# Attention scores beside the Fourier products, Hyena tables in pieces, and the experts' first block by products on TensorE

## Chip, cores and metric

The kernel runs on one core of one Trainium2 chip. The metric is the device time of one execution in microseconds: the median of several runs. Everything is computed in float32; large products are split into a high and a low part (fp32r), and three products of the parts are summed.

## The reference

Two transformer blocks, one after the other, on 512 tokens of width 1024.

- `first_block` has two layers and 256 further context tokens. Each layer takes one input projection and mixes it in three ways: attention over 8 query heads and 2 key heads (512 columns), a Fourier mix (256 columns: a 2-D DFT, then a 256x256 product), and a Hyena long convolution (256 columns: DFT of the signal and of a filter, product, inverse DFT). The output projection, a gated residual and a convolutional FFN follow. Gates and shifts come from a modulation product of the condition vector.
- `second_block` has one attention layer and a mixture of experts: each token picks one of 4 groups and 2 of its 4 experts.

```
g_weight, g_idx = lax.top_k(softmax(xf @ w_group + b_group), 1)
e_val, e_idx = lax.top_k(e_in_group, 2)
combine = sum(one_hot(expert_id) * softmax(e_val) * g_weight)
act = silu(xf @ w_gate[e]) * (xf @ w_up[e]) * combine[:, e]
out = sum over e of act @ w_down[e]
```

## The kernel before

It is written for the five engines with an explicit semaphore for every dependence; each engine executes its own list in order.

**Weights.** SyncE fetches all weight slabs (128x1024) through a ring of three (`wraw`). ScalarE makes `whi`, GpSimd `wlo` (L578), TensorE multiplies. Slabs of the modulation lie in the same ring; TensorE uses them directly in pairs (`hy_pair`, L743), and SyncE refills a slot when it is used.

**A layer's mixers.** After the input projection TensorE does the Fourier mix: L911 (`fst2`, 24 products in layer 0, 16 in layer 1), L921 (`fst3`), then the transposes of the values (L928). ScalarE evacuates to `fy` and to `hhi`; ScalarE and VectorE make `vth` and `vtl` of the values (L1570, L2126 to L2128). Attention then runs in steps, one of 128 queries against all keys of one head: `scores(i)` computes steps i and i+1 (L945), VectorE takes the minimum (L2140), ScalarE the exponential (L1585), VectorE or ScalarE divides by the sum (L2151, L1623), TensorE transposes the probabilities (L956), ScalarE and VectorE split them into `pth` and `ptl` (L1596, L2159), and TensorE multiplies by the values (L970). Loops handle two steps at a time: `scores(i)` stands ahead of `transposed(i-2)`, the outputs that are due, and `transposed(i-1)`.

**Hyena.** When attention's last output is out, ScalarE issues the tables on its own queue: `hyf512` (2 MB, into `hd5`), `hyi512` (2 MB, `hi5`) and in layer 0 `hy256` (1 MB). TensorE does `hy_pair(0)`, transposes the signal, does `hy_pair(1)` and then for each quarter of the frequencies the filter's products (L1017) and the signal's (L1029), with further pairs between them, and at the end the inverse (L1050).

**Experts.** Tokens are sorted by group into 7 blocks of 128 rows. VectorE computes the group, the place of each token (`slot_i`) and the experts' weights. GpSimd scatters the 512 rows of `xrow` to DRAM by place (L602), waits until they are there, loads block 0 (L605) and blocks 1 to 6 (L607) to `xs`, and only then starts on its share of the weight cuts (`mlo`, L611): slab 1 of experts 1 to 3 of each block. TensorE transposes block 0 (L1289), VectorE and ScalarE make `hT`, `hTh` and `hTl`, and the units start: one unit is one expert of one block, with 6 weight slabs. In a unit TensorE does `gate_up` (L1319, slabs 0 to 3) with the transposes of the last unit's activations in it (`turn_act`, L1297, behind slab 1) and `down2` of the last unit (L1337). SyncE fetches each 512 KB slab into a ring of ten (L561), ScalarE makes `mhi` (L1811), VectorE most of `mlo` (L2519).

Of the kernel before, what the change touches and what calls it, by code (L numbers as in the profile page):

```python
# [29 lines left out]
P = 128  # L30
# [118 lines left out]
def program(nc, dram, out):  # L149
# [132 lines left out]
    below = sb("below", [P, P], headones_o)  # L282
    xrow = sb("xrow", [P, TX // P, ROW], BIG)
# [19 lines left out]
    aTl = sb("aTl", [P, 2, DEXP], SCR + 13312, F32R)  # L303

# [260 lines left out]
    def _(pool):  # L565
# [9 lines left out]
        for n in range(N_SLABS):  # L575
# [13 lines left out]

            if n == B2_SLAB + IN2_T + RING - 1:  # L590
# [9 lines left out]
        pool.wait_ge(sem("routed"), 4)  # L600
# [20 lines left out]
    def _(pe):  # L621
# [174 lines left out]
        for L in range(DEPTH):  # L796
# [105 lines left out]
            pe.wait_ge(sem("fab_ready"), T // P * L + ntt)  # L902
            pe.wait_ge(sem("k_roped"), 5 * L + 5)
            for f in range(2):
                for s, c0, nt_ in fseg:
                    w = nt_ * P
                    dst = ps[:, 6 + f, 0:w] if s == 0 else ps[:, 5 - f, 0:w]
                    tb = fl5 if s == 0 else fl2
                    for q in range(nt_):
                        for ab in range(2):  # L910
                            m = pe.matmul(dst, fab[:, c0 // P + q, ab * 256 + f * P:ab * 256 + f * P + P],  # L911
                                          tb[:, ab, q, 0:w], start=q == 0 and ab == 0, stop=q == nt_ - 1 and ab == 1)
                    m.then_inc(sem("fst2"), 1)

            pe.wait_ge(sem("fy_ready"), 4 * L + 2 * len(fseg))
            for o in range(2):
                for s, c0, nt_ in fseg:
                    w = nt_ * P
                    dst = ps[:, 6 + o, 0:w] if s == 0 else ps[:, 5 - o, 0:w]
                    for f in range(2):  # L920
                        m = pe.matmul(dst, wfo[:, f, o * P:o * P + P], fy[:, f, c0:c0 + w], start=f == 0, stop=f == 1)  # L921
                    m.then_inc(sem("fst3"), 1)

            pe.wait_ge(sem("k_roped"), 5 * L + 5)
            pe.wait_ge(sem("four_out"), 4 * L + 2 * len(fseg))
            pe.wait_ge(sem("qk_lo"), 5 * L + 5)
            for tt in range(6):
                m = pe.transpose(ps[:, 4 + tt // 4, (tt % 4) * P:(tt % 4) * P + P], pxq[:, PXV, tt * P:tt * P + P],  # L928
                                 ident[:, :])
# [47 lines left out]
            for i in range(0, max(shares) + 1, 2):  # L977
                if i < N:
                    scores(i)
# [1788 lines left out]
```

## Time and profile before

| | |
|---|---|
| median of 3 runs | 2558.72 us (2557.14 to 2561.62) |
| the profiled execution | 2567.32 us, span 2565.5 us, granted clock 0.951 |
| TensorE, VectorE, ScalarE, GpSimd busy | 91%, 50%, 43%, 25% |
| chain that ended last | TensorE 77%, VectorE 12%, ScalarE 3%, DMA 2% |
| last four of 40 slices | VectorE 9, 9, 9, 8 tenths; 342, 346, 348, 270 GB/s |
| `mlo` on VectorE (L2519) | 147 x 1.451 us |
| `mlo` on GpSimd (L611) | 21 x 3.014 us |

A timeline row has the start and the duration in us, the engine, the line, the operation with its operands and count, and in brackets the idle time ahead of it with what ended it. SPq and ACTq are DMA issues on SyncE's and ScalarE's queues. A row of the chain has start, duration and the work or wait that the end went back to. A row of windows has, for each engine in the order TensorE, its weight loads, VectorE, ScalarE, GpSimd, the busy time; then the granted clock (1.00 is 2.4 GHz), the share in which the DMA engines were busy, and GB/s.

### The profile page before, as it was taken

To read this page: it belongs to the slowest core of one execution; us is meant where nothing else is said; L and a number is where in the kernel's file an instruction comes from. 1 tells how busy PE (TensorE), PEld (TensorE's weight loads), DVE (VectorE), ACT (ScalarE), POOL (GpSimd) and SP (SyncE) were. 2 spreads that over 40 slices of the span, in tenths; PEclk is the share of its full clock that TensorE was granted. 3 is DMA by queue.
4 is the path that set the end of the run, shared out by engine and by line. 5 is a ranking of instruction groups with operands and counts; after the bars stand their busy time and mean duration, and the time that the engine had idled before them with its cause. 6 is when DMAs were issued, how large, how long until landed. Compare 5 with 4: busy or idle time off the path is not lost.

```text
span 2565.5 us, 32207 instructions
## 1 busy us (share of the span) xinstructions
PE 2334.2 (91%) x12378; PEld 1861.8 (73%) x12378; DVE 1289.5 (50%) x2035; ACT 1096.9 (43%) x1687; POOL 652.5 (25%) x293
## 2 busy tenths in 40 slices
PE   4997979979999999988979888999999999959997
PEld 2875856858888788866657566888876877747776
DVE  3565932053431344236667214534524269449998
ACT  4323931353332333225357035434423268437776
POOL 1220000242222222242200034444444410212223
PEclk9999989979999999988989888999999999979999
DMA  6520032113222232112400441333332322249997
GB/s 239 190 89 22 1 117 98 58 30 118 91 66 66 83 114 75 58 50 94 140 1 33 153 144 55 94 98 98 98 97 68 100 66 59 109 162 342 346 348 270
DMA packets 81034, 291.20 MB, mean 114 GB/s; under 512 B 10713, under 2 KB 13050, under 8 KB 79932
## 3 DMA queue, kind: packets, MB, share of 16 engines
q1 hardware_dynamic: 74192, 257.68, 29.8%
q10 hardware_dynamic: 4108, 22.08, 2.3%
q0 software_dynamic: 2592, 9.48, 0.9%
q8 instruction: 96, 1.57, 0.2%
q14 instruction: 46, 0.38, 0.0%
HBM read 283.43 MB, written 9.48 MB: 114 GB/s over the span
## 4 chain that ended last, share of the span: by engine, by line
PE 77%; DVE 12%; ACT 3%; DMA 2%; issue 2%; POOL 2%; DVEq 1%; SPq 0%; ACTq 0%; POOLq 0%
PE ps L635 37%; PE ps L682 12%; DVE mlo L2519 5%; PE ps L658 3%; PE ps L970 3%; PE ps L956 2%; PE ps L1319 2%; PE ps L743 2%; PE ps L1191 2%; PE ps L945 1%; POOL x L584 1%; PE ps L1017 1%; PE ps L911 1%; PE ps L1337 1%; PE ps L1029 1%
## 5 line engine op out<-in xcount | busy, mean ns | idle before, releaser
L578 POOL TENSOR_TENSOR wlo<-wraw,whi 128x1024 fp32r<-128x1024 f32 x208 | 502.1, 2415 | 1530.0 <-ACT whi L1359 881.1
L635 PE MATMUL ps<-hhi,whi 128*128 128x512 f32 x1624 | 593.6, 366 | 3.0 <-DVE hlo L2219 2.0
L635 PE MATMUL ps<-hlo,whi 128*128 128x512 f32 x1624 | 585.3, 360 | 0.0
L635 PE MATMUL ps<-hhi,wlo 128*128 128x512 f32 x1624 | 582.5, 359 | 0.0
L635 PEld LDWEIGHTS ps<-hhi,whi 128*128 128x128 f32 x1624 | 307.6, 189 | 83.6 <-issue 31.2
L635 PEld LDWEIGHTS ps<-hhi,wlo 128*128 128x128 f32 x1624 | 306.6, 189 | 48.1
L635 PEld LDWEIGHTS ps<-hlo,whi 128*128 128x128 f32 x1624 | 307.4, 189 | 45.7 <-issue 1.0
L1942 DVE SCALAR_TENSOR_TENSOR up<-ps,cconv,up 128x511 f32<-128x511 f32 (+1 forms) x132 | 83.2, 658 | 296.3 <-ACT up L1686 293.8
L2519 DVE TENSOR_TENSOR mlo<-mraw,mhi 128x1024 fp32r<-128x1024 f32 x147 | 208.9, 1451 | 5.3 <-ACT mhi L1811 5.2
L1366 ACT ACTIVATE whi<-wraw 128x1024 fp32r<-128x1024 f32 x132 | 138.9, 1052 | 154.2 <-PE ps L682 120.3
L1686 ACT ACTIVATE up<-ps,cconv 128x768 f32<-128x768 f32 (+1 forms) x88 | 77.8, 885 | 257.6 <-PE ps L635 257.2
L682 PE MATMUL ps<-alo,whi 128*128 128x512 f32 (+1 forms) x528 | 188.0, 356 | 0.0
L682 PE MATMUL ps<-ahi,whi 128*128 128x512 f32 (+1 forms) x528 | 187.4, 355 | 0.0
L682 PE MATMUL ps<-ahi,wlo 128*128 128x512 f32 (+1 forms) x528 | 186.6, 353 | 0.0
L1811 ACT ACTIVATE mhi<-mraw 128x1024 fp32r<-128x1024 f32 x168 | 166.0, 1049 | 1.2 <-DMA mraw<-in_w_moe 1.0
L2268 DVE TENSOR_TENSOR y<-y,ps 128x768 f32<-128x768 f32 (+1 forms) x32 | 26.3, 820 | 227.6 <-PE ps L682 227.6
L1359 ACT ACTIVATE whi<-wraw 128x1024 fp32r<-128x1024 f32 x76 | 80.2, 1057 | 112.3 <-PE ps L635 86.9
L682 PEld LDWEIGHTS ps<-ahi,whi 128*128 128x128 f32 x528 | 99.6, 189 | 15.0
L682 PEld LDWEIGHTS ps<-ahi,wlo 128*128 128x128 f32 x528 | 99.2, 188 | 14.8
L611 POOL TENSOR_TENSOR mlo<-mraw,mhi 128x1024 fp32r<-128x1024 f32 x21 | 63.3, 3014 | 183.1 <-ACT mhi L1811 183.1
L682 PEld LDWEIGHTS ps<-alo,whi 128*128 128x128 f32 x528 | 99.5, 188 | 13.8
L658 PE MATMUL ps<-hhi,whi 128*128 128x512 f32 (+1 forms) x168 | 68.1, 405 | 32.4 <-DVE hlo L1920 22.9
(350 smaller groups left out, 4185.6 us busy)
## 6 DMA issues: line engine op xcount, KB each, us to landing
wraw<-in_w_all SPq DMA_DIRECT2D x288, 512.0 KB, 3.6
mraw<-in_w_moe SPq DMA_DIRECT2D x168, 512.0 KB, 5.5
mraw_b<-in_w_mod SPq DMA_DIRECT2D x10, 512.0 KB, 15.4
fl<-in_four ACTq DMA_DIRECT2D x2, 2048.0 KB, 8.2
hd<-in_hyf ACTq DMA_DIRECT2D x2, 2048.0 KB, 10.0
hi<-in_hyi ACTq DMA_DIRECT2D x2, 2048.0 KB, 15.8
slot_rows<-in_slot_rows ACTq DMA_DIRECT2D x1, 3612.0 KB, 20.6
xs<-slot_rows POOLq DMA_DIRECT2D x7, 516.0 KB, 7.2
```

Of the source, the lines that this page charges most:

```text
L578: pool.tensor_tensor(wlo[:, slot, :], wraw[:, AT_W[n] % RING, :], whi[:, slot, :].bitcast(F32), ALU.subtract).then_inc(lo_split, 1)
L611: pool.tensor_tensor(mlo2[:, n % MS, :], mraw2[:, n % MR, :], mhi2[:, n % MS, :].bitcast(F32), ALU.subtract).then_inc(pool_lo, 1)
L635: m = pe.matmul(ps[:, bank + b, 0:w], a, r[:, c0:c0 + w], start=k == 0 and q == 0, stop=k == KT - 1 and q == 2)
L658: m = pe.matmul(ps[:, bank + b, 0:w], a, r[:, c0:c0 + w], start=k == 0 and q == 0, stop=k == KT - 1 and q == 2)
L682: m = pe.matmul(ps[:, bank + b, 0:w], a, r[:, c0:c0 + w], start=k == 0 and z == 0, stop=k == PAIRS - 1 and z == 2)
L970: m = pe.matmul(ps[:, 6 + ht % 2, c0:c0 + HALF], u[:, g, kts[c], :], w[:, unit % 2, c, g * HALF:g * HALF + HALF], start=g == 0 and c == 0 ...
L1359: act.activation(whi[:, n % RING, :], wraw[:, AT_W[n] % RING, :], ACT.Copy).then_inc(hi_split, 1)
L1366: act.activation(whi[:, n % RING, :], wraw[:, AT_W[n] % RING, :], ACT.Copy).then_inc(hi_split, 1)
L1686: act.activation(up[:, p % 2, z, 0:W], psf[:, b * 512:b * 512 + W], ACT.Identity, bias=cconv[:, s, 3:4], scale=cconv[:, s, 1:2]).then_inc( ...
L1811: act.activation(mhi2[:, m % MS, :], mraw2[:, n % MR, :], ACT.Copy).then_inc(ring_hi, 1)
L1942: dve.scalar_tensor_tensor(dst[:, c0 + 1:c0 + w], ps[:, bank + b, 0:w - 1], w0, dst[:, c0 + 1:c0 + w], ALU.mult, ALU.add)
L2519: dve.tensor_tensor(mlo2[:, m % MS, :], mraw2[:, n % MR, :], mhi2[:, m % MS, :].bitcast(F32), ALU.subtract).then_inc(ring_lo, 1)
```

## The change

Three things are moved or replaced.

1. In each layer the scores, minima and exponentials of attention's steps 0 to 3 stand between and behind the two halves of L911 and their evacuations, ahead of L921 and the value transposes. The first pair is scaled there too. The main loop starts at i = 2 and computes scores from i = 4.
2. In layer 0 three of four parts of `hyf512` are loaded by GpSimd's queue while attention runs on the context queries (after 8 units of outputs); ScalarE loads the last quarter at the end of attention. In both layers `hyi512` is issued behind the first `hsp` copy, `hy256` behind the second.
3. The first block of sorted rows is no longer taken from DRAM. VectorE compares each token's place with 0 to 127 (`iota`, loaded over `rot`); TensorE forms the transposed block as products of `xrow` with these 0/1 matrices, and the rows' weights likewise, which go to `meta0`. The rows' way through DRAM stays, for all 7 blocks; block 0 from DRAM is waited for only where its result is added.

```diff
+            if n == IN_T + RING - 1:
+                pool.wait_ge(sem("o_ready"), 2 * NQT)
+                pool.dma_start(hd5[:, 0, 0:2, :], dram["hyf512"][:, 0, 0:2, :]).then_inc(sem("hfwd_early"), 16)
+                pool.dma_start(hd5[:, 1, :, :], dram["hyf512"][:, 1, :, :]).then_inc(sem("hfwd_early"), 16)
...
         pool.wait_ge(sem("slots_clear"), 16)
-        pool.wait_ge(sem("routed"), 4)
+        pool.wait_ge(sem("routed"), 5)
...
             for f in range(2):
                 for s, c0, nt_ in fseg:
...
                     m.then_inc(sem("fst2"), 1)
+                if f == 0:
+                    pe.wait_ge(sem("qk_lo"), 5 * L + 5)
+                scores(2 * f)
...
-            for i in range(0, max(shares) + 1, 2):
-                if i < N:
+            for i in range(2, max(shares) + 1, 2):
+                if 4 <= i < N:
                     scores(i)
...
                 pe.wait_ge(sem("hfwd_in"), 16 * L + 16)
+                pe.wait_ge(sem("hfwd_early"), 32)
...
+        def place_first(half, bank):
+            if half == 0:
+                pe.wait_ge(sem("routed"), 4)
+            for q in range(4):
+                k = 4 * half + q
+                for tt in range(TX // P):
+                    m = pe.matmul(ps[:, bank, q * P:q * P + P], xrow[:, tt, k * P:k * P + P], place1[:, tt, :],
+                                  start=tt == 0, stop=tt == TX // P - 1)
+            m.then_inc(sem("hT_done"), 1)
+        def place_weights():
+            pe.wait_ge(sem("routed"), 5)
+            for tt in range(TX // P):
+                m = pe.matmul(ps[:, 4, 0:ROW - D], place1[:, tt, :], xrow[:, tt, D:ROW], start=tt == 0,
+                              stop=tt == TX // P - 1)
+            m.then_inc(sem("hT_done"), 1)
...
-        turn_block(0, 0, 7)
-        turn_block(0, 1, 6)
+        place_first(0, 7)
+        place_first(1, 6)
+        place_weights()
...
+            for f in range(2):
+                for s, c0, nt_ in fseg:
...
+                    act.activation(fy[:, f, c0:c0 + w], ps[:, 6 + f, 0:w] if s == 0 else ps[:, 5 - f, 0:w],
+                                   ACT.Copy).then_inc(sem("fy_ready"), 1)
+                exponentials(2 * f)
+                exponentials(2 * f + 1)
+                if f == 0:
+                    scaled_act(1)
...
             act.wait_ge(sem("attn_out"), 2 * NQT * L + nht)
-            act.dma_start(hd5[:, :, :, :], dram["hyf512"]).then_inc(sem("hfwd_in"), 16)
-            act.dma_start(hi5[:, :, :, :], dram["hyi512"]).then_inc(sem("hinv_in"), 16)
             if L == 0:
-                act.dma_start(hd2[:, :, :, :], dram["hy256"]).then_inc(sem("hinv_in"), 16)
+                act.dma_start(hd5[:, 0, 2:4, :], dram["hyf512"][:, 0, 2:4, :]).then_inc(sem("hfwd_in"), 16)
+            else:
+                act.dma_start(hd5[:, :, :, :], dram["hyf512"]).then_inc(sem("hfwd_in"), 16)
...
                     act.activation(hsp[:, f, :], ps[:, 4 + f % 2, :], ACT.Copy).then_inc(sem("hsp_ready"), 1)
+                    if s == 0 and f == 0:
+                        act.dma_start(hi5[:, :, :, :], dram["hyi512"]).then_inc(sem("hinv_in"), 16)
+                    if L == 0 and s == 0 and f == 1:
+                        act.dma_start(hd2[:, :, :, :], dram["hy256"]).then_inc(sem("hinv_in"), 16)
...
+            minimum(0)
+            minimum(1)
+            scaled(0)
+            scaled(1)
+            minimum(2)
+            minimum(3)
...
         dve.tensor_copy(slot_i[:, :], r(8, 1, 10).rearrange("p t n -> p (t n)"))
+        for tt in range(TX // P):
+            m = dve.tensor_scalar(place1[:, tt, :], iota[:, :], rt[:, 8, tt, 10:11], None, ALU.is_equal)
+        m.then_inc(sem("routed"), 1)
...
             c = 2 + 2 * (b % 2)
+            if b == 0:
+                dve.wait_ge(sem("first_block_in"), 16)
...
         block_full(0, 0, 7)
         block_full(0, 1, 6)
+        dve.wait_ge(sem("hT_done"), 3)
+        dve.tensor_copy(meta0[:, :], ps[:, 4, 0:ROW - D])
+        dve.drain()
         block_low(0, 0)
         block_low(0, 1)
```

## Rows read from the trace of the kernel before

**Rows 1.** Timeline of TensorE, layer 0, from the Fourier products to full attention.
```profile
231.50 5.43 PE L921 MATMUL ps<-fy,wfo 128*128 128x512 f32 x16 [0.47 <-ACT fy L1555]
237.91 0.85 PE L928 MATMUL ps<-ident,pxq 128*128 128x128 f32 x6 [0.98 <-issue]
...
247.07 1.54 PE L956 MATMUL ps<-ident,pr 128*128 128x128 f32 x6 [2.77 <-DVE pr L2151]
249.42 1.52 PE L956 MATMUL ps<-ident,pr 128*128 128x128 f32 x6 [0.80 <-DVE ptl L2159]
...
256.97 0.51 PE L945 MATMUL ps<-hhi 64*128 64x512 f32 x2 [0.32 <-ACT pr L1585]
```

**Rows 2.** Timelines of ScalarE and of VectorE in the same stretch.
```profile
242.82 0.87 ACT L1570 ACTIVATE vth<-ps 128x384 fp32r<-128x384 f32 x2
...
243.83 0.38 DVE L2126 MEMSET vth<- 128x384 f32 x1 [1.95 <-ACT vth L1570]
...
245.76 0.49 DVE L2128 TENSOR_TENSOR vtl<-ps,vth 128x384 fp32r<-128x384 f32 x1
...
253.29 1.82 DVE L2140 TENSOR_REDUCE stat<-ps 128x1 f32<-128x768 f32 x2 [0.95 <-PE ps L945]
```

**Rows 3.** Windows, layer 0, ahead of the first transposes.
```profile
240.00:244.20 4.20, 1.24 (x14) 0.97 (x12) 2.20 (x3) 2.63 (x6) 0.00 (x0) 1.00 0.00 0
244.20:247.00 2.80, 0.10 (x2) 0.00 (x0) 2.63 (x9) 0.00 (x0) 0.00 (x0) 0.50 0.00 0
```

**Rows 4.** The chain that ended last, the same stretch of layer 1.
```profile
1309.32 0.84 PE ps L928 x6
...
1328.45 1.31 PE ps L945 x11
```

**Rows 5.** Layer 0, Hyena's start: issues, TensorE, a window, and the queues' packets (330 to 420).
```profile
357.20 0.35 ACTq L1628 DMA_DIRECT2D hd<-in_hyf  x1
357.62 0.81 SPq L497 DMA_DIRECT2D wraw<-in_w_all  x2
...
369.50 1.93 PE L743 MATMUL ps<-wraw,cs 128*32 128x512 f32 x8 [8.87 <-DMA wraw<-in_w_all]
...
361.00:369.50 8.50, 0.00 (x1) 0.04 (x2) 0.00 (x0) 0.05 (x1) 0.00 (x0) 0.65 0.99 419
...
q1 hardware_dynamic: 1728, 6.29, 19.3%
q10 hardware_dynamic: 432, 5.24, 14.5%
```

**Rows 6.** Layer 1, Hyena's start: SyncE's issues and TensorE.
```profile
1404.23 0.33 SPq L497 DMA_DIRECT2D wraw<-in_w_all  x1
1408.40 1.93 PE L743 MATMUL ps<-wraw,cs 128*32 128x512 f32 x8 [1.80 <-DMA wraw<-in_w_all]
...
1426.83 0.80 SPq L497 DMA_DIRECT2D wraw<-in_w_all  x2
1430.58 1.06 PE L743 MATMUL ps<-wraw,cs 128*32 128x512 f32 x8 [0.16 <-DMA wraw<-in_w_all]
```

**Rows 7.** Timelines at the experts' start: TensorE, GpSimd, VectorE.
```profile
2295.75 1.97 PE L1289 MATMUL ps<-ident,xs 128*128 128x128 f32 x8 [23.77 <-DMA xs<-slot_rows]
...
2308.96 0.38 PE L1297 MATMUL ps<-ident,eact 128*128 128x128 f32 x2
...
2277.73 1.40 POOL L602 DMA_INDIRECT slot_rows<-xrow,slot_i  x1 [39.12 <-DVEq L2512]
...
2292.60 3.18 POOL L607 DMA_DIRECT2D xs<-slot_rows  x6
2301.09 2.49 POOL L611 TENSOR_TENSOR mlo<-mraw,mhi 128x1024 fp32r<-128x1024 f32 x1 [5.30 <-ACT mhi L1811]
...
2276.93 4.63 DVE L2519 TENSOR_TENSOR mlo<-mraw,mhi 128x1024 fp32r<-128x1024 f32 x4
```

**Rows 8.** The experts' stage: the page's group of L2519; landing of the slabs from 2300 on.
```profile
L2519 DVE TENSOR_TENSOR mlo<-mraw,mhi 128x1024 fp32r<-128x1024 f32 x147 | 208.9, 1451 | 5.3 <-ACT mhi L1811 5.2
...
DMA to landing us min/median/max: 3.5/5.5/7.2
```

More of the change, by code:

```diff
@@ L900, in _ @@
                 m.then_inc(sem("fst1"), 1)
[L902 to L929, printed above, removed]
-            m.then_inc(sem("vt_done"), 1)
             steps = attn_steps(L)
@@ L1548, in _, with exponentials, scaled_act @@
                    .then_inc(sem("qk_hi"), 1)
+            act.activation(consts[:, 15:16], zero_c, ACT.Exp)
+            steps = attn_steps(L)
+            hv, before = halves(L)
+            shares = output_shares(L)
+            N = len(steps)
+            units = 0
+            def exponentials(i):
+                nk = len(steps[i][4]) * P
+                act.wait_ge(sem("min_ready"), STEPS0 * L + i + 1)
+                if i >= 4:
+                    act.wait_ge(sem("t_ready"), HALVES0 * L + before[i - 3])
+                act.activation(pr[:, i % 4, 0:nk], psf[:, 1024 * (i % 2):1024 * (i % 2) + nk], ACT.Exp,
+                               bias=stat[:, i % 4, 0:1], scale=-1.0, accum_out=stat[:, i % 4, 1:2])\
+                   .then_inc(sem("exp_done"), 1)
+            def scaled_act(i):
+                nk = len(steps[i][4]) * P
+                act.wait_ge(sem("inv_ready"), STEPS0 * L // 2 + i // 2 + 1)
+                act.activation(pr[:, i % 4, 0:nk], pr[:, i % 4, 0:nk], ACT.Copy, scale=stat[:, i % 4, 2:3])\
+                   .then_inc(sem("p_scaled"), 1)
             n = 0
@@ L2110, in _, with minimum, scaled @@
                 dve.drain()
+            steps = attn_steps(L)
+            hv, before = halves(L)
+            shares = output_shares(L)
+            N = len(steps)
+            units = 0
+            def minimum(i):
+                nk = len(steps[i][4]) * P
+                dve.wait_ge(sem("s_ready"), STEPS0 * L + i + 1)
+                dve.tensor_reduce(stat[:, i % 4, 0:1], psf[:, 1024 * (i % 2):1024 * (i % 2) + nk], AX_X, ALU.min)\
+                   .then_inc(sem("min_ready"), 1)
+            def scaled(i):
+                nk = len(steps[i][4]) * P
+                dve.wait_ge(sem("exp_done"), STEPS0 * L + i + 1)
+                m = dve.reciprocal(stat[:, i % 4, 2:3], stat[:, i % 4, 1:2])
+                if i % 2:
+                    m.then_inc(sem("inv_ready"), 1)
+                    return
+                dve.drain()
+                dve.tensor_scalar(pr[:, i % 4, 0:nk], pr[:, i % 4, 0:nk], stat[:, i % 4, 2:3], None, ALU.mult)\
+                   .then_inc(sem("p_ready"), 1)
+            minimum(0)
[4 more added lines that the diff above has]
+            minimum(3)
             fseg = hsegs[L]
@@ L2162, in transposed_lo @@
                        .then_inc(sem("pt_lo"), 1)
-            for i in range(0, max(shares) + 1, 2):
-                if i < N:
+            values_lo()
+            for i in range(2, max(shares) + 1, 2):
+                if 4 <= i < N:
                     minimum(i)
                     minimum(i + 1)
-                if i == 0:
-                    values_lo()
                 if 2 <= i < N + 2:
@@ L2522, in block_full @@
         def block_full(b, half, bank):
-            dve.wait_ge(sem("hT_done"), 2 * b + half + 1)
+            dve.wait_ge(sem("hT_done"), 2 * b + half + (2 if b else 1))
             q = slice(4 * half, 4 * half + 4)
```

96 lines of the change are left out of this document (42 added, 54 removed).

## The prediction

> **What bounds the kernel now.** I read the page first: TensorE is busy for 91% of the span, and 77% of the chain that ended last is its own work. So a change pays only where TensorE stands idle on the chain, or where another engine sets the pace. I then went through three places that the diff touches, in order of time, each with the timeline of one engine at a time, and asked of every idle stretch of TensorE who ended it.
>
> *Attention's start, in both layers.* After the Fourier products (L911, L921) TensorE has little to do while the first softmax steps pass through VectorE and ScalarE: it turns the values at 237.91, does two pairs of scores, and waits 2.77 us for `pr` before the first transposes at 247.07; the pipeline is full only at 256.97 [rows 1]. The wait is filled by VectorE: four clears and two differences for `vtl`, 243.83 to 246.25 [rows 2]. Meanwhile the granted clock falls to 0.50, that is 1.2 GHz [rows 3]. Layer 1 does the same, 1309.32 to 1328.45 [rows 4].
>
> *The Hyena tables.* In layer 0 TensorE waits 8.87 us at 369.50 for a pair of modulation slabs that SyncE had asked for at 357.62, right behind ScalarE's 2 MB table of 357.20 and two more; the DMA engines are full, at 419 GB/s [rows 5]. In layer 1 the same pair, asked for ahead of the tables at 1404.23, is there at 1408.40 [rows 6].
>
> *The experts' start.* TensorE waits 23.77 us until the first block of sorted rows is back from DRAM: four scatters from 2277.73, their landing, and the load [rows 7]. From there to the end VectorE sets the pace: its 147 cuts fill 208.9 us with 5.3 us of idle time ahead of them, and the weights land in 3.5 to 7.2 us, with no queue building up [rows 8]. So what this stage starts earlier it should end earlier.
>
> **Part A, scores of steps 0 to 3 beside the Fourier products.** TensorE's work is the same, reordered. A group of score products takes 1.31 us [rows 4]; two such groups now stand ahead of the value transposes, 2.6 us, less the 0.47 us wait ahead of L921 that they cover. VectorE and ScalarE do the first two minima, exponentials and scalings under the second half of L911, where nothing of theirs was due. The second pair of exponentials now stands in ScalarE's queue ahead of the evacuations of L921; two minima (1.82 us [rows 2]) and two exponentials end about 2.8 us after the second scores, while L921 itself takes 5.43 us, so only early evacuations wait, nobody for long. If that cover failed, it would cost up to the two exponentials, some 1.8 us a layer. The values are turned at 237.91 + 2.6 - 0.5 = 240.0, plus 0.85, 0.87 for `vth` and 2.42 for `vtl` [rows 1, 2]: the first transposes start at 244.15 in place of 247.07, 2.9 us earlier. Behind them the minima of steps 2 and 3 no longer stand ahead of the low parts, 0.3 us more. What is late next is no longer `pr` but `vtl`, and then the same ping-pong of transposes, low parts, minima and exponentials. The clock decides the rest: if it is low there as before, the gain stays at 3.2 us; if it stays high, the next score group takes its 1.31 us and not twice that, each set of transposes some 0.8 and not 1.54 us [rows 1, 4], and I get 4.9. TensorE is still idle for over 4 of the 5 us ahead of 244, much as it was ahead of the fall at 244.2 [rows 1, 3], so I take the low clock and 3.3 a layer: **6.6 us**, bounds 3 and 10.
>
> **Part B, the tables.** 1.5 MB of the forward table go out on GpSimd's queue once eight heads' outputs are done (`o_ready`), some 25 us before they are needed. GpSimd pays two issues of 0.53 us (six took 3.18 [rows 7]); queued behind its wait is the split of the next slab, which is not due before the output projection, so nothing; without that cover 1.1 us. At the end of attention 0.5 MB is left in front of the pair. Alone the pair took 4.17 us [rows 6]; 0.5 MB more at 419 GB/s is 1.25 us, so it lands at 357.62 + 5.4 = 363.0, and TensorE gains 6.5 us. The pair's products, the turn and the first filter products ran at the low clock and still will. The cost: the inverse table (2 MB) is now issued after the first `hsp` copy, about 3.8 us ahead of the fetch of pair 3, which TensorE wants 3.6 us later; without other traffic it lands just in time, 1426.83 to 1430.58 with 0.16 us of waiting [rows 6]. With the table beside it some 0.5 MB and the pair share 419 GB/s: 1.2 us later at least, 2.1 if the two share evenly to the end; I take 1.6 in each layer. In layer 1 nothing is gained for it. ScalarE's issues are 0.35 us each [rows 5], ahead of copies due 3 us later: nothing. Sum 6.5 - 1.6 - 1.6 = 3.3 us, **3.3 us**, bounds -2 and 7.
>
> How large packets weigh is seen in the same rows: around those tables one queue moved 5.24 MB in 432 packets and the other 6.29 MB in 1728, 12.1 KB against 3.6 KB [rows 5]. In the Trainium skill, "DMA: Bandwidth & Descriptors", section "Queues, rings and completion order", each DMA engine takes whole packets from its queues in turn. By that the slabs had a quarter of the rate, 3.6 / 15.7, and 1.05 MB would take about 11 us; the trace has 11.9 us from 357.62 to 369.50, so it agrees. For pair 3 the rule gives the same 2 us, since only the tail of the table is left.
>
> **Part C, the first block by products.** Removed from TensorE's path: the wait for the DRAM trip, and eight transposes (1.97 us). Added: four comparisons on VectorE, 128x128 each, between nothing and 0.38 us apiece (the clear of 128x384 [rows 2]); I take 0.2, 0.8 us in all, which delays GpSimd's scatters too, since they wait for the weights computed behind. 32 placing products of 128 columns and four for the weights follow. Products of 128-column f32 tiles that aren't transposes aren't in this place of the trace; if each runs as two passes of the transposes' 0.25 us (1.97 / 8, low clock), 72 passes are 18 us, at the high clock 9; as single passes half of these. I take 10 us, a start at the low clock that rises on the way: done at 2276 + 10 = 2286, then the last `hT`, the copy of the weights' columns and two `hTl`: first expert product at about 2287.5 instead of 2299.1. VectorE's first cuts (4.63 us from 2276.93) lie beside it.
>
> But this isn't what the stage gains. GpSimd still has its whole way in front of its first cut, for expert 1 slab 1: four scatters, their landing, seven loads issued until 2295.8, all 0.8 us later now, then a cut of 2.49 us [rows 7]. So `mlo` of that slab is there at 2296.6 + 2.5 = 2299.1. TensorE reaches it at about 2287.5 + 5.5 + 1.4 = 2294.4 and stands. With six products at the low clock again (2.6 us) the turn of expert 0's activations (L1297) comes at 2301.7 instead of 2308.96, 7.3 us earlier; at the high clock 8.5. VectorE has done the same cuts by then in both cases and waits for that turn; from there it is full. I take **7.4 us**, bounds 4 (placing 18 us, or loads of the later blocks late at the second expert pair) and 12 (GpSimd's cut not waited for).
>
> A rule speaks against this part: the Trainium skill, "SBUF — State Buffer", section "A bandwidth-pool intuition that's wrong (but worth ruling out)", puts a core's share of HBM at about 358 GB/s and calls HBM almost always the end-to-end bottleneck. The experts stream at 342 to 348 GB/s on the page, so by it the stage would be bound by loads; the trace speaks against it with 419 GB/s in layer 0 [rows 5].
>
> **Sum.** 6.6 + 3.3 + 7.4 = 17.3 us. The profiled execution took 2567.3 us (span 2565.5), so 2550.0 for it; it stands 8.6 above the median of the runs, and the parts are all waits of one kind, so I take the same 17.3 off the median of 2558.7: **2541.4 us**.
>
> **Rivals.**
> *Every cover holds and the clock stays up*: A 10, B 3.3, C 12, 25.3 us less, 2533.4. For it: only one engine has to be quicker in each place. Against: GpSimd's queue order is fixed by the code, and the clock fell at 244.2.
> *Transfers take it back*: pair 3 waits 4 us in each layer (the 8.87 us wait shows how badly a pair can fare), B -1.5, and C 4: 9.1 us less, 2549.6. For it: large packets ahead of small ones. Against: most of the table has passed by then.
> *The experts are bound by their loads*: C is 0, as the loads already begin at 2278 and can't end sooner; 9.9 us less, 2548.8. For it: DMA engines over 90% busy. Against: landings of 3.5 to 7.2 us and VectorE's full row [rows 8]. This is what the skill's HBM rule would do here.
> *The change does nothing*: what TensorE gains at each place it waits again for another engine, under 5 us; A 3, B -2, C 4 would be 2553.7, the lowest of all bounds.
> *Slower: the low clock stays in the experts' stage.* The stage's 266 us hold 28 units, 9.5 us each. A start in pieces (products, a stand of some 5 us for GpSimd, products) might leave TensorE at 1.2 GHz; each unit at that clock costs up to 9.5 us more, and from two units on it takes everything back: three units give 2570. Against it: in all three places TensorE was back at the high clock within about 5 us of steady work.
>
> **How the numbers follow.** Forecast, own range 2536 to 2547: 0.58. All covers 0.12. Transfers 0.12. Loads 0.11. Nothing 0.05. Slower 0.02. The 0.8 range reaches to the all-covers case on one side and past transfers and loads on the other, 2533 to 2551. A measurement of this kernel can tell about 0.2%, 5 us, from no change: faster by more, 0.93; within, 0.05; slower, 0.02.
>
> **What would show it.** A: the first transposes of attention about 3 us after the end of `vth`, released by `vtl`, and steps 6 on some 3 us nearer to the end of L921's part than 19.1 us plus two score groups would put them. B: the wait at the second pair in layer 0 under 3 us; a new wait of 1 to 2 us at pair 3 in both layers. C: a stand of TensorE some 4 to 5 us long, released by GpSimd's `mlo`, in expert 1, and L1297 to the end of the span as long as before, 256.5 us. The forecast is wrong if that last length grows (loads or clock), if the placing products take over 15 us, or if the values aren't turned until L921's evacuations have waited for the exponentials.

## The result and the profile after

| | before | after |
|---|---|---|
| median of the runs | 2560.17 us, 6 runs (2553.83 to 2566.85) | 2546.64 us, 6 runs (2539.59 to 2553.14) |
| the profiled execution | 2567.32 us, span 2565.5 us | 2553.14 us, span 2551.3 us |

The ratio is 0.9947, with an interval of 0.9928 to 0.9967: 13.5 us between the medians, 14.2 us between the two profiled spans (each profiled execution is some 7 us above its median). A second comparison of the same two kernels gave 0.9944 (0.9927 to 0.996). The forecast was 17.3 us off and 2541.4, with a range of 2536 to 2547. 2546.6 lies in it by 0.4 us; the second comparison's 2547.8 would lie just outside.

To see where the time went, I cut both timelines at products that both kernels have and took the distances. "Without" and "with" are means over all profiled kernels, those of the experiments below too, that lack the part in question (three) or have it and nothing else that touches the stretch (ten for attention, eight for the tables, four for the experts).

| stretch of TensorE's timeline | before | after | without | with |
|---|---|---|---|---|
| layer 0: first L911 (L941) to last attention output (L970, L985) | 142.3 | 140.5 | 142.5 | 140.1 |
| layer 1: first L911 (L941) to first attention output | 42.5 | 40.7 | 42.4 | 38.4 |
| layer 0: last attention output to last inverse product (L1050, L1066) | 82.8 | 79.6 | 82.7 | 78.6 |
| layer 1: the same | 64.0 | 63.7 | 63.0 | 64.0 |
| router (L1269, L1285) to first turn of an expert's result (L1297, L1325) | 40.6 | 33.9 | 40.3 | 33.4 |
| that turn to the end | 256.5 | 258.9 | 256.4 | 258.3 |

So part A gave 2.4 + 4.0 = 6.4 us (forecast 6.6), part B 4.1 - 1.0 = 3.1 (3.3), part C 6.9 - 1.9 = 5.0 (7.4). Single profiles scatter around these means. In layer 1 the attention stretch is 37.4 to 40.7 us with part A and 40.8 to 43.8 without, and the Hyena stretch 62.8 to 65.5 with part B and 61.5 to 64.0 without; in layer 0 the Hyena stretch is 76.9 to 79.7 with part B and 82.2 to 82.9 without. So the gains by part are known to 1 or 2 us each, and the -1.0 is within the scatter. The long stretches between, whose code is the same, differ by 4 and by 6 us from profile to profile (845 to 849 us, and 796 to 802), in both directions.

**Attention, layer 0**: TensorE's timeline of the kernel after, which answers to [rows 1], then two rows of ScalarE's.
```profile
237.97 5.43 PE L954 MATMUL ps<-fy,wfo 128*128 128x512 f32 x16
244.38 0.84 PE L961 MATMUL ps<-ident,pxq 128*128 128x128 f32 x6 [0.98 <-issue]
248.84 0.45 PE L971 MATMUL ps<-ident,pr 128*128 128x128 f32 x1 [3.62 <-DVE vtl L2197]
...
258.06 0.80 PE L928 MATMUL ps<-hhi 64*128 64x512 f32 x2
...
240.84 0.86 ACT L1617 ACTIVATE hhi<-ps 128x512 fp32r<-128x512 f32 x2
242.57 0.60 ACT L1617 ACTIVATE hhi<-ps 128x512 fp32r<-128x512 f32 x1 [0.86 <-PE ps L954]
```
The rows of ScalarE are its evacuations of L954. The first two of them stand behind the exponentials until 240.84, but from the third on ScalarE waits for TensorE again, so nothing behind them came late. The first transposes come 4.46 us behind the turn of the values (9.16 in [rows 1]) and their releaser is `vtl`. The scores of step 6 come 13.7 us behind the turn, not 19.1.

**Hyena, layer 0 and layer 1**: TensorE's timeline of after, the waits for slabs, which answer to [rows 5] and [rows 6].
```profile
363.52 1.93 PE L755 MATMUL ps<-wraw,cs 128*32 128x512 f32 x8 [3.07 <-DMA wraw<-in_w_all]
...
376.64 3.72 PE L1033 MATMUL ps<-hpm,hd 128*128 128x256 f32 x16
382.60 1.06 PE L755 MATMUL ps<-wraw,cs 128*32 128x512 f32 x8 [2.24 <-DMA wraw<-in_w_all]
383.59 5.41 PE L1045 MATMUL ps<-hut,hd 128*128 128x256 f32 x16
...
1423.25 1.07 PE L755 MATMUL ps<-wraw,cs 128*32 128x512 f32 x8 [2.27 <-DMA wraw<-in_w_all]
```
The 8.87 us wait at the second pair is 3.07 us. A new wait of 2.24 us stands at the third pair, in layer 1 2.27 us where [rows 6] had 0.16. Over all eight profiles with part B as it was, this wait is 1.57 to 2.42 us in layer 0 and 1.76 to 2.53 in layer 1. Behind it L1045 takes 5.41 us here, at the low clock, where the like group ahead of it takes 3.72; that happened behind 7 of these 16 waits.

**The experts' start**: TensorE and GpSimd of after, which answer to [rows 7].
```profile
2266.03 9.99 PE L1299 MATMUL ps<-place,xrow 128*128 128x128 f32 x64 [3.94 <-DVE place L2541]
2275.85 0.96 PE L1307 MATMUL ps<-xrow,place 128*128 128x8 f32 x8
2277.83 0.50 PE L1347 MATMUL ps<-mhi,hTh 128*128 128x512 f32 x1 [1.02 <-DVE hTl L2582]
2289.68 0.79 PE L1347 MATMUL ps<-mhi,hTh 128*128 128x512 f32 x1 [4.74 <-POOL mlo L623]
2292.40 0.63 PE L1325 MATMUL ps<-ident,eact 128*128 128x128 f32 x2
...
2268.60 1.32 POOL L614 DMA_INDIRECT slot_rows<-xrow,slot_i  x1 [39.88 <-DVEq L2561]
...
2283.35 0.58 POOL L617 DMA_DIRECT2D xs<-slot_rows  x1 [8.69 <-DMA slot_rows<-xrow,slot_i]
2283.92 3.20 POOL L619 DMA_DIRECT2D xs<-slot_rows  x6
```
The placing takes 10.8 us; the trace has two entries for each float32 product, so 64 and 8 entries are 32 and 4 products. The first expert product comes 19.3 us behind the router's products instead of 30.7. Then TensorE stands for 4.74 us until GpSimd, back from the scatters and the seven loads, has cut its slab: the stand that the forecast named, at its forecast length (3.97 us in after_again and 4.11 in c_only).

What follows the turn of expert 0's result (2292.40) decides what the stage gains: SyncE's issues, ScalarE and VectorE of after, then VectorE of before.
```profile
2289.65 3.29 SPq L568 DMA_DIRECT2D mraw<-in_w_moe  x7
...
2297.38 1.06 ACT L1851 ACTIVATE mhi<-mraw 128x1024 fp32r<-128x1024 f32 x1 [2.98 <-DMA mraw<-in_w_moe]
2298.98 1.06 ACT L1851 ACTIVATE mhi<-mraw 128x1024 fp32r<-128x1024 f32 x1 [0.54 <-DMA mraw<-in_w_moe]
...
2298.47 1.22 DVE L2568 TENSOR_TENSOR mlo<-mraw,mhi 128x1024 fp32r<-128x1024 f32 x1 [2.82 <-ACT mhi L1851]
2301.21 0.48 DVE L2595 SCALAR_TENSOR_TENSOR eact<-ps,meta,esil 128x256 f32<-128x256 f32 x1
```
```profile
2311.00 4.87 DVE L2519 TENSOR_TENSOR mlo<-mraw,mhi 128x1024 fp32r<-128x1024 f32 x3 [0.42 <-ACT mhi L1811]
2315.79 0.47 DVE L2546 SCALAR_TENSOR_TENSOR eact<-ps,xs,esil 128x256 f32<-128x256 f32 x1
```
VectorE makes the second expert's activations (`eact`) 8.8 us behind the turn, in the kernel before 6.8 us behind it. Ahead of them in its queue stand cuts that wait for ScalarE's `mhi`, and ScalarE waits for slabs. SyncE refills the ring in order, and the slot of GpSimd's slab is next: it issued nothing for 10 us, and then seven fetches in 3.3 us from 2289.65 on, when GpSimd's cut was done. The first of them landed 7.7 us later, beside the sorted rows, the last of which landed at 2298.1.

It is the same in after_again, whose turn is at 2286.52: ScalarE's wait, and a product of TensorE right behind the turn (0.40 us at the full clock, 0.63 at the low one).
```profile
2291.72 1.06 ACT L1851 ACTIVATE mhi<-mraw 128x1024 fp32r<-128x1024 f32 x1 [3.30 <-DMA mraw<-in_w_moe]
...
2287.11 0.40 PE L1347 MATMUL ps<-mlo,hTh 128*128 128x512 f32 x1
```

### The profile page after: what moved, and what is told of

Its sections match the earlier page's. It is cut to its first block, busy times and chain, and to the rows that moved or that the text cites. A ratio compares the mean times of both kernels' runs of the same rounds, so it can differ in the third digit from the quotient of the medians.

```text
span 2551.3 us, 32346 instructions
## 1 busy us (share of the span) xinstructions
PE 2343.3 (92%) x12442; PEld 1869.8 (73%) x12442; DVE 1285.1 (50%) x2040; ACT 1099.0 (43%) x1687; POOL 652.1 (26%) x295
## 3 DMA queue, kind: packets, MB, share of 16 engines
q8 instruction: 96, 1.57, 0.2%
## 4 chain that ended last, share of the span: by engine, by line
PE 77%; DVE 11%; ACT 3%; DMA 2%; POOL 2%; issue 2%; DVEq 1%; SPq 0%; POOLq 0%; ACTq 0%
PE ps L647 37%; PE ps L694 12%; DVE mlo L2568 5%; PE ps L670 4%; PE ps L985 3%; PE ps L971 2%; PE ps L1347 2%; PE ps L755 2%; PE ps L1207 2%; PE ps L928 2%; POOL x L591 1%; PE ps L941 1%; PE ps L1045 1%; PE ps L1066 1%; DMA wraw<-in_w_all 1%
## 5 line engine op out<-in xcount | busy, mean ns | idle before, releaser
L623 POOL TENSOR_TENSOR mlo<-mraw,mhi 128x1024 fp32r<-128x1024 f32 x21 | 62.8, 2990 | 177.0 <-ACT mhi L1851 177.0
## 6 DMA issues: line engine op xcount, KB each, us to landing
mraw_a<-in_w_mod SPq DMA_DIRECT2D x6, 512.0 KB, 10.5
```

Source lines behind the costliest of these rows:

```text
L623: pool.tensor_tensor(mlo2[:, n % MS, :], mraw2[:, n % MR, :], mhi2[:, n % MS, :].bitcast(F32), ALU.subtract).then_inc(pool_lo, 1)
```

## Experiments

### One part at a time

Each of these is the kernel before with one part of the diff. `a_only` has the attention part:

```diff
             for f in range(2):
...
+                if f == 0:
+                    pe.wait_ge(sem("qk_lo"), 5 * L + 5)
+                scores(2 * f)
```

> The kernel before with part A alone (scores of steps 0 to 3 beside the Fourier products). Theory: each layer gains 3.3 us between the start of L911 and the first output product of attention, since the wait for the first transposes shrinks: 45.3 us becomes 42 in layer 0, 42.5 becomes 39 in layer 1, and the whole kernel is 6 to 7 us faster (ratio 0.9975). In the changed kernel the profile had only 0.3 and 1.8 us of it; the theory says that 1.9 and 1.3 us went to a low clock at the start of L911, which comes from where the clock's fall happens to lie, not from the change, so it should come and go between profiles. Rival: the scores between the halves of L911 themselves cost the clock or the time, in every profile; then this kernel shows 45 and 40.7 us again and gains 2 us (ratio 0.9992).

Measured: 2555.83 us against 2562.7, ratio 0.997 (0.9957 to 0.9983), 6.9 us less; in the profile 3.1 us off layer 0's stretch and 4.9 off layer 1's. The low clock at the start of L911 is absent here, as the theory allows; b_only has it without part A, so the rival, that the scores between the halves cost it, is out.

`b_only` has the tables:

```diff
+                pool.dma_start(hd5[:, 0, 0:2, :], dram["hyf512"][:, 0, 0:2, :]).then_inc(sem("hfwd_early"), 16)
+                pool.dma_start(hd5[:, 1, :, :], dram["hyf512"][:, 1, :, :]).then_inc(sem("hfwd_early"), 16)
...
+                    if s == 0 and f == 0:
+                        act.dma_start(hi5[:, :, :, :], dram["hyi512"]).then_inc(sem("hinv_in"), 16)
```

> The kernel before with part B alone (Hyena's tables in pieces). Theory: in layer 0 the stretch from the last output product of attention to the last inverse product shrinks from 82.8 us by about 3: 6.7 gained at the second pair of modulation slabs, 2.1 lost at the pair fetched beside the inverse table, some lost to the clock there. In layer 1, 64.0 us stay within 0.5: 1.4 gained at the forward table, 2.1 lost at that pair. Whole kernel 3 us faster (ratio 0.9988), nearly all in layer 0. Rival: the wait at the pair in layer 1 isn't the inverse table's doing; then it stays near 0.2 us here, and layer 1 gains 2 us too.

Measured: 2560.23, ratio 0.9993 (0.9978 to 1.0007), which can't be told from no change. Its profile shows 78.2 us in place of 82.8 in layer 0 and 65.5 in place of 64.0 in layer 1. The wait at layer 1's third pair is there, 2.16 us, so the rival is out.

`c_only` has the experts' first block:

```diff
-        turn_block(0, 0, 7)
-        turn_block(0, 1, 6)
+        place_first(0, 7)
+        place_first(1, 6)
+        place_weights()
```

> The kernel before with part C alone (first block by products). Theory: expert 0's activations are turned 6.5 us earlier as counted from the group decision (L1269): 40.6 us become 34; from there to the end it takes some 2.4 us more than 256.5, because SyncE's fetches stand in order behind GpSimd's first cut and ScalarE waits for slabs. Net 4 us (ratio 0.9984). Rival: the 2.4 us are scatter between executions; then the end is 256.5 us after the turn and the kernel gains 6.5 us (ratio 0.9975).

Measured: 2555.49, ratio 0.9972 (0.9957 to 0.9987), 7.2 us less. In its profile the turn comes 33.5 us behind the router and the end 257.5 us behind the turn, 1.1 more than without part C where the theory had 2.4. The waits that the theory named are there: ScalarE waits 3.29 us for a slab behind the turn. The three parts sum to 16.6 us; together they gave 12 to 14. Each difference is uncertain by 3 to 5 us, so this doesn't show that they get in each other's way, nor that they don't.

### GpSimd's cut ahead of its wait (`after_cut`)

If GpSimd's queue sets the experts' start, its cut of expert 1's slab should be taken out from behind the scatter's landing and the loads.

```diff
-        pool.wait_ge(sem("rows_placed"), 16 * (TX // P))
-        pool.dma_start(xs[:, 0, :], slots_d[0:P, :]).then_inc(sem("first_block_in"), 16)
-        for b in range(1, BLOCKS):
-            pool.dma_start(xs[:, b, :], slots_d[b * P:b * P + P, :]).then_inc(sem("blocks_in"), 16)
-        for u, j in M_POOL:
+        for q, (u, j) in enumerate(M_POOL):
             n = M_AT[(u, j)]
+            if q == 1:
+                pool.wait_ge(sem("rows_placed"), 16 * (TX // P))
+                pool.dma_start(xs[:, 0, :], slots_d[0:P, :]).then_inc(sem("first_block_in"), 16)
+                for b in range(1, BLOCKS):
+                    pool.dma_start(xs[:, b, :], slots_d[b * P:b * P + P, :]).then_inc(sem("blocks_in"), 16)
```

> The changed kernel with one move on GpSimd's queue: its first cut (expert 1, slab 1) stands right behind the four scatters, ahead of the wait for their landing and of the seven block loads. Theory (GpSimd's queue sets the experts' start): TensorE's 4.7 us stand before that slab goes away, expert 0's activations are turned some 5 us earlier than in the changed kernel (29 us from the group decision in place of 34), SyncE's fetches go on earlier as well, so the end comes 5 to 7 us earlier: ratio to the kernel before 0.992 to 0.993. Rival (the experts' stage is bound by its loads): the turn comes earlier but the end doesn't, and the time is that of the changed kernel (0.9947), with longer waits of ScalarE for slabs. A third: the loads of the later blocks, now some 2.5 us later at most, stop TensorE at the second block instead and take 1 to 3 us of the gain.

Measured: 2555.78, ratio 0.9982 (0.9967 to 0.9996), slower than the changed kernel. TensorE's timeline, and the page's group of the loads of the sorted rows (count, KB each, median us from issue to landing), of after_cut:
```profile
2302.01 1.09 PE L1318 MATMUL ps<-ident,xs 128*128 128x128 f32 x4 [13.67 <-issue]
...
xs<-slot_rows POOLq DMA_DIRECT2D x7, 516.0 KB, 13.1
```
The stand for GpSimd is gone, and the turn of expert 0's result comes 6.3 us earlier, 27.6 us behind the router. But at the third expert TensorE turns the first half of block 1, and its wait asks for the loads of blocks 1 to 6 together. The cut ahead has freed SyncE's ring earlier, so these loads now share the DMA engines with more weights and take 13.1 us instead of 6.9: TensorE stands for 13.67 us. (The row names no releaser. The last of the loads landed at 2301.9, and cut_blk below takes the wait away.) The theory held for the turn and failed for the end; the third expectation was right in kind, but the stop costs far more than 1 to 3 us.

### The changed kernel again (`after_again`)

> The changed kernel as it is, beside the next three, so that they have one yardstick. The first comparison gave 0.9947 of the kernel before, with 0.9928 to 0.9967; single stages differ between profiles by 1 to 2 us from the clock that a stage happens to start at. Expected again: 0.993 to 0.997, some 2545 to 2553 us.

Measured: 2547.76, ratio 0.9944 (0.9927 to 0.996). This is the yardstick of the next three, which ran beside it.

### The inverse table one step earlier (`after_tab`)

```diff
             rows(HY_G[L], 3)
+            act.dma_start(hi5[:, :, :, :], dram["hyi512"]).then_inc(sem("hinv_in"), 16)
...
-                    if s == 0 and f == 0:
-                        act.dma_start(hi5[:, :, :, :], dram["hyi512"]).then_inc(sem("hinv_in"), 16)
```

> The changed kernel with one move: in each Hyena layer ScalarE issues the DMA of the inverse tables right after the third set of rows, before the first half's spectrum, and not behind it. What it is meant to tell: whether the two waits that were late next (TensorE's wait for the third pair of weight slabs, about 2 us in layer 0 and 2.1 us more than before in layer 1) come from where this 1 MB stands among the weight fetches. If so, the stretch from the last output product to the last inverse product falls from 79.6 to about 76 to 77 us in layer 0 and from 63.7 to 62 us or so in layer 1, and the kernel is 3 to 5 us faster than the changed one. The rival: it is the total of the bytes on full DMA engines, not their order; then the wait only moves to an earlier pair of slabs, the two stretches stay within 1 us, and the time stays.

(The table has 2 MB, not 1.) Measured: 2539.93, ratio 0.9928 (0.9911 to 0.9945), 7.8 us less than the changed kernel beside it (the two intervals overlap a little; the stretches below account for 6.3). ScalarE's issue and TensorE's third pair in layer 0, of after_tab:
```profile
362.61 0.37 ACTq L1671 DMA_DIRECT2D hi<-in_hyi  x1
...
377.32 1.06 PE L755 MATMUL ps<-wraw,cs 128*32 128x512 f32 x8
378.32 3.72 PE L1045 MATMUL ps<-hut,hd 128*128 128x256 f32 x16
```
No wait at the pair, and L1045 at 3.72 us. In after the same issue stands 8.8 us behind the second pair:
```profile
372.30 0.36 ACTq L1679 DMA_DIRECT2D hi<-in_hyi  x1
```
Here it stands 2.0 us behind it (at 360.62), and most of the table has passed when the third pair is fetched. Layer 0's stretch is 75.4 us and layer 1's 60.9, against 78.6 and 64.0 on average with part B as it was: 3.2 and 3.1 us, more than the waits alone because the low clock behind them is gone too. The rival, that only the sum of the bytes counts, is out.

### Block 1 awaited by itself (`cut_blk`), and loaded by itself (`cut_one`)

`cut_blk` is after_cut with

```diff
-                pool.dma_start(xs[:, 0, :], slots_d[0:P, :]).then_inc(sem("first_block_in"), 16)
-                for b in range(1, BLOCKS):
+                pool.dma_start(xs[:, 1, :], slots_d[P:2 * P, :]).then_inc(sem("first_block_in"), 16)
+                for b in (0, *range(2, BLOCKS)):
...
-            pe.wait_ge(sem("blocks_in"), 16 * (BLOCKS - 1))
+            pe.wait_ge(*((sem("first_block_in"), 16) if b == 1 else (sem("blocks_in"), 16 * (BLOCKS - 1))))
```

> GpSimd's first cut ahead of its wait for the scatter (as in after_cut) and two semaphores for the loads of the sorted rows: block 1, which TensorE wants first, is issued first and awaited alone; the six others follow at once and are awaited together only at the turn of block 2, four experts later. Theory: in after_cut the early cut took 5.6 us off the turn and 13 us came back because TensorE's first turn of block 1 stood for all six loads together, which took 13 us each beside the weight fetches. Then the wait for block 1 falls from 13.7 us to under 6 us, and from the last router step to the end it takes 284 to 288 us (292.8 in the changed kernel, 299.5 in after_cut), 5 to 8 us less than the changed kernel. Rival: the experts' stage is bound by the bytes of the weights, so that what is gained at its head is lost later in it, wherever the blocks stand: 291 to 294 us from the router to the end.

Measured: 2545.97, ratio 0.9947 (0.9932 to 0.9963). The 13.67 us wait is gone, and from the router to the end it takes 287.8 us (292.8 in after). The median is only 1.8 us below the changed kernel's beside it: the profiled execution is the fastest of its five, so the 5 us hold for the stage and aren't shown for the whole. `cut_one` has one line more, ahead of the loop over the six other blocks:

```diff
+            if q == 2:
```

> As cut_blk, but the six other blocks are issued only behind GpSimd's second cut, one expert later, so block 1's 128 rows share the DMA engines with the weight fetches alone. Theory: block 1 lands in 5 to 8 us instead of about 13, its wait is gone or under 2 us, and the stretch from the router to the end is 1 to 3 us shorter than with cut_blk. Rival (bytes bound the stage): same as cut_blk and the changed kernel, 291 to 294 us. If the cause were not the shared semaphore but the cut itself moving ahead, both would stay near after_cut's 299.5 us.

Measured: 2541.36, ratio 0.9924 (0.9907 to 0.994), and 289.4 us from the router to the end. By these stretches that is no gain on cut_blk, so my expectation of 1 to 3 us less isn't borne out. But each is from one profile, 1.1 us of the 1.6 between them lies in the last expert, and the medians say 4.6 us less, with intervals that overlap: whether cut_one is faster stays open. What was left is seen in cut_blk: windows (the last three columns are the granted clock, the DMA share and GB/s), and ScalarE's timeline.
```profile
2291.00:2296.00 5.00, 3.34 (x17) 2.64 (x17) 1.65 (x2) 2.86 (x4) 2.39 (x1) 1.00 1.02 409
2296.00:2301.00 5.00, 3.43 (x18) 2.60 (x17) 3.84 (x5) 4.34 (x5) 0.00 (x0) 1.00 1.04 413
...
2288.39 1.06 ACT L1852 ACTIVATE mhi<-mraw 128x1024 fp32r<-128x1024 f32 x1 [1.50 <-DMA mraw<-in_w_moe]
2290.95 1.06 ACT L1852 ACTIVATE mhi<-mraw 128x1024 fp32r<-128x1024 f32 x1 [1.50 <-DMA mraw<-in_w_moe]
2293.51 1.06 ACT L1852 ACTIVATE mhi<-mraw 128x1024 fp32r<-128x1024 f32 x1 [0.71 <-DMA mraw<-in_w_moe]
```
TensorE is busy for 3.4 of 5 us, VectorE for 1.7 and 3.8, and the DMA engines are full. A weight slab arrives each 2.56 us; an expert needs six in 8.3 to 9.8 us, one each 1.5 us. Loaded one expert later, in cut_one, the six blocks take the same transfer time from the next expert: its third expert takes 10.5 us and its fourth 12.3 us, 22.8 together, where cut_blk has 13.6 and 8.7, 22.3 together (distances between VectorE's products for `eact`, L2595 of after).

### The loads spread over the experts (`spread`)

```diff
+            b = {1: 1, 2: 0, 3: 2, 6: 3, 9: 4, 12: 5, 15: 6}.get(q)
+            if b is not None:
+                landed = sem("first_block_in") if b % 2 else sem("blocks_in")
+                if b // 2:
+                    pool.wait_ge(landed, 16 * (b // 2))
+                pool.dma_start(xs[:, b, :], slots_d[b * P:b * P + P, :]).then_inc(landed, 16)
```

> As cut_blk, but the seven blocks of sorted rows (0.53 MB each) are not loaded together: block 1 ahead of GpSimd's second cut, block 0 ahead of the third, and blocks 2 to 6 one by one, each shortly before the four experts that read it, 36 us apart. Theory (bytes): from 2286 us to about 2312 us cut_blk's DMA engines are full, at 410 GB/s, and a weight slab lands each 2.56 us, where the stage later takes one each 1.5 us and its engines are at 0.95 with 345 GB/s; 2.6 MB moved out of that stretch at 410 GB/s are 6.5 us, of which the stage should get back 3 to 6 us: from the router to the end 282 to 285 us against 287.8 in cut_blk. Rival (the stage cannot use earlier slabs, its rhythm is that of TensorE): 287 to 289 us, as cut_blk.

Measured: 2538.54, ratio 0.9917 (0.99 to 0.9934); 284.2 us from the router to the end, 3.6 less than cut_blk. ScalarE's timeline of spread at the like place:
```profile
2290.18 1.06 ACT L1855 ACTIVATE mhi<-mraw 128x1024 fp32r<-128x1024 f32 x1 [0.21 <-DMA mraw<-in_w_moe]
2291.50 1.05 ACT L1855 ACTIVATE mhi<-mraw 128x1024 fp32r<-128x1024 f32 x1
2292.75 1.06 ACT L1855 ACTIVATE mhi<-mraw 128x1024 fp32r<-128x1024 f32 x1 [0.20 <-DMA mraw<-in_w_moe]
```
The slabs come each 1.3 us. The third expert takes 9.5 us, as in the settled rhythm. The bytes of the sorted rows were the bound there.

### The placing made twice (`place_twice`)

```diff
-            for q in range(4):
+            for q in (0, 1, 2, 3, 0, 1, 2, 3):
```

> The changed kernel with the 64 placing products made twice, into the same banks, so the output is the same. It measures what the placing itself costs on the path. 64 products took 9.99 us, the first few at the low clock; 64 more are 9 to 10 us. In the changed kernel the experts' products then stand 4.7 us for GpSimd's cut of expert 1, which is set by the scatter and not by TensorE. Theory (GpSimd's queue sets the start): the first expert product is 9 to 10 us later, that wait is gone, and the turn of the first expert's result comes only 4 to 5.5 us later; from the router to the end 297 to 298 us against 292.8. Rival (the placing is on the path in full): turn and end 9 to 10 us later, 302 us. Rival (bytes bound the head of the stage, so that neither matters much): the turn is later by 4 to 5 us and the end by under 3 us, 294 to 296 us.

Measured: 2546.58 (two runs), ratio 0.9943 (0.9924 to 0.9962), the changed kernel's. The group of the placing grows from 9.99 to 17.17 us, the first expert product comes 26.5 us behind the router instead of 19.3, the turn of expert 0's result 34.8 instead of 33.9, and the end 292.6 instead of 292.8. All three expectations missed by the number, the third by least: 32 more products (64 more entries) cost 0.9 us at the turn and nothing that shows at the end or in the time (known to 5 us). The windows of after around the stand for GpSimd, then two of place_twice at the like place:
```profile
2284.90:2289.60 4.70, 0.03 (x1) 0.00 (x0) 2.36 (x2) 2.02 (x3) 4.70 (x7) 0.89 0.95 351
2289.60:2295.00 5.40, 5.32 (x14) 4.16 (x15) 1.00 (x2) 1.33 (x2) 2.35 (x2) 0.50 1.01 405
```
```profile
2283.00:2288.00 5.00, 5.00 (x25) 4.12 (x24) 5.00 (x6) 4.82 (x7) 0.16 (x1) 1.00 1.01 403
2288.00:2293.00 5.00, 5.00 (x24) 4.01 (x23) 5.00 (x5) 2.61 (x5) 3.29 (x1) 1.00 1.03 421
```
In both kernels GpSimd's cut ends 31 us behind the router. The changed kernel comes there 4.7 us early, stands, and then runs 14 entries in 5.4 us at half the clock; place_twice comes just in time and runs 24 or 25 in 5 us at the full one. At a spacing of 0.43 us in place of 0.23, these 5.4 us hold about 2.5 us (an estimate) that the stand costs TensorE beyond itself, some 1.2 of it ahead of the turn and 1.4 behind it. The part behind the turn reaches nobody: in both kernels VectorE then waits for slabs (ScalarE waits 2.98 and 0.54 us for them in after, 0.89 and 1.49 in place_twice), and `eact` of the second expert comes 42.7 and 42.5 us behind the router. Arriving early bought nothing.

### All together (`best`)

It is spread with after_tab's edit.

> All that helped together: the changed kernel with the inverse tables' DMA of each Hyena layer issued behind the third set of rows, GpSimd's first cut ahead of its wait for the scatter, block 1 awaited by itself and the other blocks' loads spread over the experts. If the parts add up: after_tab took 6 to 7 us off the changed kernel, cut_blk about 5 us from the router to the end, spreading 3 to 5 us more: 2530 us or so, 0.987 to 0.990 of the kernel before. Rival: gains of single stages are lost in the next one, as the cut's was; then 0.992, no better than the better of its parts.

Measured: 2535.23 us, ratio 0.9899 (0.9883 to 0.9915), 25.7 us less than before and the fastest of all; expected were 2530 or so. Its stretches are 75.6 and 61.0 us in the two Hyena layers and 283.6 us from the router to the end. It is 3.3 us below spread, where the table alone had brought 7.8; the two intervals overlap, so how much of the table's gain is kept is known to 2 or 3 us only. Its Hyena stretches are those of after_tab (75.4 and 60.9).

## Why the prediction was right, and where a term was off

- **A, 6.6 us: 6.4.** The steps held: `vtl` ends the wait, the transposes are 4.5 us behind the turn (forecast 4.1), and of the evacuations only the first two stand behind the exponentials. The two layers are not alike (2.4 and 4.0). In layer 0 one reason is the clock, which the sum had the same before and after. In eight of the thirteen profiles, after among them, the first 24 entries (12 products) of L911 or L941 took 10.53 us, with a granted clock of 0.69 from 217 to 222 us in after; in the other five, before among them, 8.83 or 8.86. Part A isn't the cause: b_only hasn't got it and took 10.53, a_only and spread have it and took 8.83, and from there to the first output it took them 42.1 us instead of 45.0. Compared like with like, part A gives 3.1 us in layer 0 (142.2 and 142.3 against 139.2 twice) where that group is fast and 2.5 where it is slow (143.0 in b_only against 140.4 to 140.7), near the 3.3 of the forecast.
- **B, 3.3 us: 3.1.** The second pair waits 3.07 us, where 2.4 were forecast, and 5.8 us of its wait are gone. The wait at the third pair is 2.24 and 2.27 us in after, just above the "1.2 to 2.1" of the prediction, and in layer 0 of after it costs 1.7 us more through the clock in L1045, a term that the sum lacked; against that stands a shorter wait for the forward table in layer 1 (2.19 us against 3.40 before). By stretches layer 0 gained 4.1 us (forecast 4.9) and layer 1 lost 1.0 (1.6). That the sum agrees to 0.2 us is luck: the two errors cancel, and neither is known that well. The Trainium skill, "DMA: Bandwidth & Descriptors", section "Queues, rings and completion order", has the engines take whole packets from the queues in turn; by that the 2 MB table, in large packets, delays slabs that are fetched right behind it. after_tab agrees: 6.8 us more of a head start take the wait away.
- **C, 7.4 us: 5.0.** The turn came 6.9 us earlier (forecast 7.3), the stand was 4.74 us (forecast 4.7), the placing 10.8 (10 taken). The step that failed is "L1297 to the end of the span as long as before", and under it "from there it is full", said of VectorE: 256.5 us became 258.3 on average, 258.9 in after. By the second expert's activations 2.0 us are lost, 8.6 to 9.4 us behind the turn in the four profiles in place of 6.8, because VectorE's cuts wait for slabs, as shown above. TensorE's low clock behind the stand isn't the reason: it reaches past the turn in after, but in after_again and c_only TensorE is at the full clock from the turn on, and there the activations are 9.4 and 8.6 us behind it. Where GpSimd's cut is moved ahead and SyncE isn't held up (after_cut, cut_blk, cut_one, spread, best), they are 7.3 us behind it. From there on, the last expert takes 5.4 us instead of 4.3 in after and after_again (1.1 us lost), but 4.3 in after_tab and c_only, and the rhythm between gives 0.7 us back. The 5.4 us occur in five of the ten profiles with part C and in none of the three without; what makes them wasn't followed up. The forecast had let the stage count as moved once its first event is.
- **The rivals.** Loads as the bound: not up to the turn, which came as early as forecast, nor from the third expert on, whose rhythm is that of before; but in between, slabs asked for late and landing beside the sorted rows took 2.0 us back. And it is the next bound: with the cut ahead, the blocks' loads cost what spread gave back. All covers at a high clock: out, GpSimd's cut was waited for. Transfers: right in kind, the third pair waits in both layers, but 2.2 us and not 4. No effect: out, all three places moved. Slower: the clock was back after 5.4 us.
- On the Trainium skill's share of HBM, about 358 GB/s ("SBUF — State Buffer", section "A bandwidth-pool intuition that's wrong (but worth ruling out)"): the windows above show 409 to 421 GB/s for one core over 5 us, so the measurement decides.

## What to carry to other kernels

Moving the start of a stage is worth what the slowest of its suppliers allows: find the next releaser before making the first one faster, and ask what else it is queued behind. The first event of a stage can come early and its second not: follow the gain to the next engine that waits. A wait that asks for a set of transfers, of which one is needed, is a debt that shows only when the stage starts earlier. Loads needed over a long stage should be spread over it, and a large table issued well ahead of the small fetches that are due, not just ahead of them.

## What was not expected of the hardware

- An idle stretch costs TensorE more than itself: after 4.7 us of standing it worked for 5.4 us at half the clock. A kernel with 7.2 us more of useless products in that gap was no slower.
- A wait of 1.98 to 2.00 us ahead of the first Fourier products was followed by the low clock in eight profiles (10.53 us for 24 entries) and not in four (before, a_only, c_only, spread: 8.83 us). Waits of 1.57 to 2.53 us at the third pair were followed by it in 7 cases of 16. What decides it, these runs don't show.
- Seven loads of 516 KB took 6.9 us (median) in after and 13.1 in after_cut, issued together both times, and 7.7 in spread, issued one by one. In after_cut SyncE's fetches weren't held up beside them.
